# Closing stage of a hybrid decoder step: the samples' gates multiplied in one piece, their copies ahead of a weight split, and the prompt columns of unit 0 ahead of the sample columns

## The reference

```python
o = jax.nn.sigmoid(ga) * o_a + jax.nn.sigmoid(gb) * o_b
h = x + jnp.einsum('bte,ed->btd', o, w_o)
hn = rmsnorm(h, mlp_g)
y = h + jnp.einsum('btf,fd->btd', jnp.square(jax.nn.relu(jnp.einsum('btd,df->btf', hn, w_up))), w_down)
```

## Time and profile before

| | us |
|---|---|
| median of 3 runs | 1647.08 |
| lowest, highest | 1645.26, 1650.61 |
| profiled execution | 1650.32 |
| its span | 1648.6 |
| TensorE busy, share of the span | 1528.9, 93% |
| TensorE weight loads busy | 1257.7, 76% |
| VectorE busy | 834.8, 51% |
| ScalarE busy | 596.4, 36% |
| GpSimd busy | 193.8, 12% |

### The profile page before, as it was taken

The page is one execution under the profiler, slowest core; times in us unless marked ns, Lnnn a source line. Parts: engine busy times, 40 slices in busy tenths (PEclk is TensorE's granted clock), DMA queues, the critical chain, the costliest instruction groups (busy, mean ns, idle before and its releaser), DMA issues. The chain is left out here.

```text
span 1648.6 us, 31808 instructions
## 1 busy us (share of the span) xinstructions
PE 1528.9 (93%) x12584; PEld 1257.7 (76%) x12584; DVE 834.8 (51%) x1812; ACT 596.4 (36%) x1162; POOL 193.8 (12%) x287
## 2 busy tenths in 40 slices
PE   7999999999999999989887999498968999999998
PEld 5888888878899957656555555366648999999998
DVE  4866623216998588867752232254544432234322
ACT  5332211325555377667642121133333331133210
POOL 1010000001443000844210000000000000000000
PEclk9999999999999989998988999699978999999999
DMA  7634478434343473335237865899864343434321
GB/s 207 200 118 168 169 267 289 155 92 101 102 126 102 121 215 95 128 112 150 78 113 269 287 241 181 288 362 346 304 236 158 102 127 102 127 102 127 103 76 55
DMA packets 189482, 276.27 MB, mean 168 GB/s; under 512 B 36781, under 2 KB 118125, under 8 KB 189238
## 3 DMA queue, kind: packets, MB, share of 16 engines
q1 hardware_dynamic: 172834, 223.08, 41.8%
q0 software_dynamic: 8352, 33.73, 6.5%
q10 hardware_dynamic: 8180, 17.91, 3.0%
HBM read 249.50 MB, written 44.69 MB: 178 GB/s over the span
## 5 line engine op out<-in xcount | busy, mean ns | idle before, releaser
L799 PE MATMUL pj_ps<-all_hi,pj_xh 128*128 128x512 f32 x480 | 192.0, 400 | 0.4 <-DVE all_lo L671 0.4
L801 PE MATMUL pj_ps<-all_hi,pj_xl 128*128 128x512 f32 x480 | 189.8, 396 | 0.0
L800 PE MATMUL pj_ps<-all_lo,pj_xh 128*128 128x512 f32 x480 | 189.8, 395 | 0.0
L2815 DVE COPY de_slot<-de_ps_t 128x512 f32<-128x512 f32 (+5 forms) x117 | 69.6, 602 | 199.5 <-PE de_ps_t L2483 128.3
L2700 ACT ACTIVATE de_slot<-de_ps_t 128x512 f32<-128x512 f32 (+3 forms) x123 | 63.1, 517 | 265.1 <-PE de_ps_t L2483 147.7
L3284 PE MATMUL fi_ps<-fi_th,fi_wh 128*128 128x272 f32 x512 | 150.0, 293 | 3.3 <-DVE fi_tl L3099 3.3
L3286 PE MATMUL fi_ps<-fi_th,fi_wl 128*128 128x272 f32 x512 | 150.3, 294 | 0.0
L3285 PE MATMUL fi_ps<-fi_tl,fi_wh 128*128 128x272 f32 x512 | 149.4, 292 | 0.0
L3285 PE MATMUL fi_ps<-fi_fl,fi_wh 128*128 128x272 f32 x512 | 148.5, 290 | 0.0
L3284 PE MATMUL fi_ps<-fi_fh,fi_wh 128*128 128x272 f32 x512 | 147.8, 289 | 0.0
L3286 PE MATMUL fi_ps<-fi_fh,fi_wl 128*128 128x272 f32 x512 | 147.7, 288 | 0.0
(11 more groups left out here) (415 smaller groups left out, 3286.4 us busy)
## 6 DMA issues: line engine op xcount, KB each, us to landing
de_dv<-in_cache_diff SPq DMA_DIRECT2D x64, 512.0 KB, 9.0
all_big<-in_w_in SPq DMA_DIRECT2D x14, 2048.0 KB, 10.5
de_dk<-in_cache_diff SPq DMA_DIRECT2D x48, 512.0 KB, 9.7
all_big<-in_cache_nsa SPq DMA_DIRECT2D x64, 256.0 KB, 6.9
all_big<-in_w_up SPq DMA_DIRECT2D x16, 1024.0 KB, 6.1
all_big<-in_w_down SPq DMA_DIRECT2D x16, 1024.0 KB, 5.6
all_dk<-in_cache_diff SPq DMA_DIRECT2D x16, 512.0 KB, 6.6
all_win<-in_cache_win SPq DMA_DIRECT2D x32, 256.0 KB, 8.8
```

Of the source, the lines that this page charges most:

```text
L799: pe.matmul(ps[:, t, :], xh[:, k, xk], wh[:, u, k, :], start=k == 0, stop=False)
L800: pe.matmul(ps[:, t, :], xh[:, k, xk], wl[:, u, k, :], start=False, stop=False)
L801: return pe.matmul(ps[:, t, :], xl[:, k, xk], wh[:, u, k, :], start=False, stop=k == KT - 1)
L2815: ins = nc.vector.tensor_copy(slot[rows, g % 4, cols], ps_t[rows, g % 3, cols])
```

## The change

SP loads `ga`, `oa` and `gb` of both column halves at the beginning, and only `ob` after the last difference is stored. VectorE multiplies `ga` by `oa` once on all 64 partitions (`first_samples`), right behind the low parts of prompt tile 0. It makes the second product and the sum on 64 partitions too, behind the low parts of tile 3; GpSimd multiplies nothing there any more, and its semaphore goes. ScalarE copies the turned samples ahead of `split(1)` and VectorE takes note of the copies ahead of its own `split(1)`. TensorE makes the 240 prompt columns of the second token half of unit 0 ahead of the samples' projection, part 0 before the samples' turn and part 1 behind it, and the 32 sample columns of both parts once the samples are normalised.

```diff
@@ SP
+            for k in range(2):
+                for j, name in enumerate(("ga", "oa", "gb")):
+                    sp.dma_start(more[k][:, j, :], d[name][SEQ:TOKENS, CW * k:CW * (k + 1)]).then_inc(sample_in[0], 16)
             sp.wait_ge(last_out, 1)
...
             sp.wait_ge(last_stored, 64)
             for k in range(2):
-                for j, name in enumerate(("ga", "oa", "gb", "ob")):
-                    sp.dma_start(more[k][:, j, :], d[name][SEQ:TOKENS, CW * k:CW * (k + 1)]).then_inc(sample_in[k], 16)
+                sp.dma_start(more[k][:, 3, :], d["ob"][SEQ:TOKENS, CW * k:CW * (k + 1)]).then_inc(sample_in[1], 16)
@@ GpSimd
-            for k in range(2):
-                b = more[k]
-                pool.wait_ge(sample_in[k], 64)
-                nc.gpsimd.tensor_tensor(b[:, 2, :], b[:, 2, :], b[:, 3, :], ALU.mult).then_inc(second_part, 1)
@@ ScalarE
+            copy_samples()
             split(1)
-            copy_samples()
@@ VectorE
-            def merge_samples(k):
-                b = more[k]
-                dve.wait_ge(sample_in[k], 64)
-                step(nc.vector.tensor_tensor(b[:, 0, :], b[:, 0, :], b[:, 1, :], ALU.mult))
-                dve.wait_ge(second_part, k + 1)
-                nc.vector.tensor_tensor(b[:, 0, :], b[:, 0, :], b[:, 2, :], ALU.add).then_inc(merged, 1)
+            def first_samples():
+                dve.wait_ge(sample_in[0], 96)
+                step(nc.vector.tensor_tensor(gated[:, 0, :], gated[:, 0, :], gated[:, 1, :], ALU.mult))
+
+            def merge_samples():
+                dve.wait_ge(sample_in[1], 32)
+                step(nc.vector.tensor_tensor(gated[:, 2, :], gated[:, 2, :], gated[:, 3, :], ALU.mult))
+                nc.vector.tensor_tensor(gated[:, 0, :], gated[:, 0, :], gated[:, 2, :], ALU.add).then_inc(merged, 1)
...
             low_parts("h", 0)
+            first_samples()
             normalize(2)
...
             normalize(3)
-            for k in range(2):
-                merge_samples(k)
             low_parts("h", 3)
+            merge_samples()
+            samples_copied()
             split(1)
-            samples_copied()
             add_samples()
@@ TensorE
-            def up(u, f, b):
+            def up(u, f, b, tok=None):
+                tok = tok or halves[b]
+                out = ps[:, 2 * f + b, tok.start - PAIR * b:tok.stop - PAIR * b]
...
                 for k in range(KT):
-                    ins = product(ps[:, 2 * f + b, 0:PAIR], k, KT, b, hi, lo, th, tl)
+                    ins = product(out, k, KT, tok, hi, lo, th, tl)
...
             up(0, 1, 0)
+            pe.wait_ge(t_lo, TURN["h", 3, 1] + 1)
+            up(0, 0, 1, slice(PAIR, SEQ))
             turn("o", QT)
+            up(0, 1, 1, slice(PAIR, SEQ))
             project_samples()
             turn("h", QT)
             pe.wait_ge(t_lo, len(TURNS))
-            up(0, 0, 1).then_inc(up_done, 1)
-            up(0, 1, 1).then_inc(up_done, 1)
+            for f in range(2):
+                up(0, f, 1, slice(SEQ, TOKENS)).then_inc(up_done, 1)
```

More of the change, by code:

```diff
@@ L90 @@
     "down_done", "h_added", "h_sq", "h_root", "relued", "f_hi", "f_lo", "y_added", "f_made0", "f_made1", "y_turned",
-    "y_ready", "y_out", "window_kept", "last_sq", "last_root", "last_out", "last_stored", "dve_step", "zeroed",
-    "second_part")
+    "y_ready", "y_out", "window_kept", "last_sq", "last_root", "last_out", "last_stored", "dve_step", "zeroed")
 class Space:
@@ L2955, in finish @@
         last_sq, last_root, last_out, last_stored = (s.sem(n) for n in ("last_sq", "last_root", "last_out", "last_stored"))
-        step_sem, zeroed, second_part = (s.sem(n) for n in ("dve_step", "zeroed", "second_part"))
+        step_sem, zeroed = (s.sem(n) for n in ("dve_step", "zeroed"))
         block = ctx.enter_context(nc.Block())
@@ L3262, in turn @@
                     else:
-                        pe.wait_ge(merged, k + 1)
+                        pe.wait_ge(merged, 1)
                         src = more[k][:, 0, :]
@@ L3280, in project_samples, with product @@
                 ins.then_inc(o_done, 1)
-            def product(o, k, n_k, b, hi, lo, a_hi, a_lo):
-                tok = slice(PAIR * b, PAIR * (b + 1))
+            def product(o, k, n_k, tok, hi, lo, a_hi, a_lo):
                 pe.matmul(o, hi[:, k, :], a_hi[:, k, tok], start=k == 0, stop=False)
@@ L3286, in product @@
                 return pe.matmul(o, lo[:, k, :], a_hi[:, k, tok], start=False, stop=k == n_k - 1)
-            def up(u, f, b):
+            halves = [slice(PAIR * b, PAIR * (b + 1)) for b in range(2)]
+            def up(u, f, b, tok=None):
+                tok = tok or halves[b]
+                out = ps[:, 2 * f + b, tok.start - PAIR * b:tok.stop - PAIR * b]
                 hi = wh[:, u, :].rearrange("p (k c) -> p k c", k=KT)[:, :, P * f:P * (f + 1)]
@@ L3308, in down_products @@
                     for b in range(2):
-                        ins = product(ps[:, 4 + 2 * u + b, 0:PAIR], k, FT, b, hi, lo, fh, fl)
+                        ins = product(ps[:, 4 + 2 * u + b, 0:PAIR], k, FT, halves[b], hi, lo, fh, fl)
                 return ins
```

## The result

The kernel after took 1655.67 us, the median of 20 runs (1647.18 to 1663.29). The kernel before, in 20 runs beside them, took 1646.56 (1636.01 to 1650.61). The ratio of after to before is 1.0054, with a 95% interval of 1.0042 to 1.0066. The whole interval lies above 1.003, beyond the 0.3% that the prediction took for the least that can be told from no change, so the kernel became slower, by 9.1 us.

What follows compares the result with a forecast made beforehand. TensorE's stream from unit 1 on was taken to set the end, so its start counts: +5.6 - 0.6 + 10.2 - 8.5 + 2.4 = +9.1 us, 1656.1 against the median; range 1653.5 to 1658.5, with rivals 1650.3 to 1660.0.

Steps and rivals of the forecast that it cites:

- The merge, the split and the copies: Samples' gates merged on 64 VectorE partitions, piece split behind the samples' copies: cost 0 on the time.
- The -0.6: Ahead of the samples' projection: TensorE's wait for VectorE, 0.61 us, goes: -0.6 us.
- The early loads: Six loads issued behind the gain's, awaited by VectorE's first multiplication: cost 0, at worst some 2.5 us late.
- 240 columns: 48 matmuls of 240 columns at full clock, in front of the projection: 0.116 us each, +5.6 us (5.1 to 10.4).
- 32 columns: 48 matmuls behind the normalised samples, bound by weight loads at half clock: 0.213 us each, +10.2 us.
- The clock: TensorE, nearly idle 6.28 us before the 48 matmuls of 32 columns, runs them at 0.50; they don't raise it.
- The tail: Unit 1 starts at half clock, its first 24 matmuls taking some 5.4 us: +2.4 us (0 to 3.4).
- three signs: Wrong if the 48 take 5 us or less, clock is 1.00 within them, or unit 1 starts before 1266.
- A: Rival on the 32-column matmuls: rounded form loads weights in 0.107 us at half clock; +4.0, 1651.1 us; chance 0.12.
- B: Rival: clock comes up within the 48 small matmuls, unit 1 starts at full clock; +4.4, 1651.5 us; chance 0.07.
- C: Rival: moving columns set the price, the 48 take 1.3 us, clock survives; -2.2, 1644.9 us; chance 0.04.
- D: Rival: prompt columns below 256 at unrounded rate, or early loads late; another 4.8 or 2.5, 1661.0 or 1658.7; chance 0.07.

## Why the prediction was right

**The bound.** It was right that whatever moves the start of unit 1 moves the end: the opening and the clock's tail add up to 8.9 us, and the stretch from the stage's first instruction to the end grew by the same 8.9.

**The merge, the split and the copies** at 0 agree with the runs as far as these can tell: the kernel with them alone has a ratio of 1.0002, within some 4 us. The -0.6 was a right number with a wrong cause. The prediction put the end of TensorE's wait down to the copies coming ahead of the split. With that alone the wait stays at 0.61; it goes with the column split, whose 24 matmuls stand in its place. So in after the number holds, and as a gain of the reordering it doesn't exist.

**The early loads** were put at 0 with a bound of 2.5. They cost 1.3 in after's profiled execution and about 0.5 in the kernel with the same loads alone. In after it was the gain that came late (2.07 in place of 0.79), and VectorE's later gap took up the 0.44 us of waiting and the 0.68 of work behind it; where the wait was 0.93, it took up only a part. The landing was forecast by the 1.9 us of the earlier trace rows, at 4.5 to 6.8 us after the stage's first instruction. The multiplication that waited for them began at 10.3 in after and 9.6 in the other, and the loads of `gb` took 6.2 us in after. So 0 was somewhat too low.

**240 columns** were taken at 0.116, from the row of 256. The step is 0.111, and 0.111 at 208 too, so the columns weren't the bound any more. A step by the weight load (0.107 to 0.112) would have been the better reading. That the +5.0 came out all the same is in part luck: 48 steps of 0.111 are 5.3 us, and the rest of the 5.65 that the two blocks took (2.77 and 2.88, to the start of what follows) lies at their ends, which the prediction didn't count.

**32 columns** were taken at 0.213, and measured 0.2135. The step that carried it was to read the load from rows of the unrounded form and to justify this by the equal length of the loads. The half-width loads show it directly, for the half clock. The Trainium skill ("TensorE: Matmul & The Clock Gate", section "LDWEIGHTS (loading the stationary operand)") gives 128 weight columns an estimate of 0.107 us. That agrees with the 0.112 at full clock here and is half of what half clock shows. Its rule that the weight columns count agrees at half clock, with 0.107 for 64 and 0.213 for 128; at full clock no run varied them.

**The clock.** That the 48 run at half clock and don't raise it was right. The reason given first, the gap of 6.28 us, held in after, where the clock fell within the gap. It was only half of it: with the gap filled the clock fell within the 48 all the same. The tail was mis-sized, 1.5 us in place of 2.4, since the clock rose after 3.3 us of unit 1 and not 5.4. In the other kernels with 48 few-column matmuls this stretch was 4.2, 2.9, 3.3 and 5.2 us. It differs though the work is the same, and the two blocks of before could only bound it.

**The total.** That 9.1 was forecast and 9.1 measured is in part luck. Of the terms, the gain (+1.3) and the first block, where the clock rose sooner (-0.6), weren't in the sum, and the tail was 0.9 shorter; the three nearly cancel.

**The rivals.** A falls with the 0.2135 and the half-width loads, B with the 20.5 us at 0.50, C with the 64 columns at an unchanged price. The part of D on 240 columns falls with the 0.111; the part on late loads shows once, at half its size. Of the three signs that the prediction named for its failure two stayed away. The third, unit 1 before 1266, is met to the letter by 1263.96, but only because the whole stage began 6.4 us earlier. Counted from the stage's start it is 1270.4 beside the forecast 1269.7. An absolute time was a poor sign; it should have been a distance from the stage's start. Of the things it expected to see, the first block came 1.3 us late by the same count, and the half clock lasted 3.3 us into unit 1 and not some 5.

## What to carry to other kernels

Splitting the columns of a group of matmuls repeats every weight load: ask what the smaller part costs in weight columns, and at which clock it will run, before counting what it puts ahead of a wait. Here few-column matmuls kept TensorE busy in the profile and still ran at half clock, they and the first microseconds of what followed. To fill a wait, use wide matmuls, and time them: a shorter opening in one profile isn't yet a gain. Of the five kernels here that put work into the wait and left the second half whole, one was clearly faster than before.

## What the runs showed of the hardware

- In this rounded form a matmul with 128 weight columns took 0.111 to 0.112 us at full clock for 32, 208 and 240 moving columns, and 0.213 at half clock for 32 and 64. With 64 weight columns and 32 moving ones it took 0.107 at half clock.
- The clock fell from 1.00 to 0.50 with TensorE without a gap, 2.72 us into 32-column matmuls, and stayed at 0.50 through 20.5 us of them, each in one execution. The Trainium skill ("TensorE: Matmul & The Clock Gate", section "HAM oscillation — how this bites in real kernels") tells of such falls where small tiles leave TensorE waiting for data; here nothing was waited for.
- VectorE's operation on 512 float32 columns took 0.68 us on 32 partitions and 0.67 to 0.68 on 64.
- The earlier stages differ between executions of kernels that are alike up to there: the closing stage started anywhere from 1209.7 to 1220.0 us, and TensorE had spent some 72 to 109 us at half clock before 1200 us. This spread hides changes of 2 to 4 us in a single profiled execution.
